# Attention scores as three products of split operands in place of one float32 product

## The reference, cut to what matters

```python
s = jnp.einsum('bqhmd,bkhmd->bhmqk', qb, kb, preferred_element_type=jnp.float32) * scale
s = jnp.where(causal, s, -jnp.inf)
prob = jax.nn.softmax(s, axis=-1)
attn = prob[:, :, 0] - lam * prob[:, :, 1]
outs.append(jnp.einsum('bhqk,bkhe->bqhe', attn.astype(v.dtype), vb))
```

## Time and profile before

| | |
|---|---|
| median of 3 runs | 3677.48 us (3675.54 to 3686.17) |
| the profiled execution | 3677.04 us, its span 3675.3 us |
| PE busy | 3268.1 us, 89% of the span |
| DVE, ACT, POOL busy | 1364.8, 978.2, 864.1 us |
| mean granted TensorE clock | 0.95 of full |
| attention stage, from the first load's issue to the last scores | about 782 to 1245 us of the span |

### The profile page before, as it was taken

The page is one execution under the profiler, slowest core; times in us unless marked ns, Lnnn a source line. Parts: engine busy times, 40 slices in busy tenths (PEclk is TensorE's granted clock), DMA queues, the critical chain, the costliest instruction groups (busy, mean ns, idle before and its releaser), DMA issues. The chain is left out here.

```text
span 3675.3 us, 70085 instructions
## 1 busy us (share of the span) xinstructions
PE 3268.1 (89%) x26336; PEld 2299.8 (63%) x26337; DVE 1364.8 (37%) x2425; ACT 978.2 (27%) x2040; POOL 864.1 (24%) x1064
## 2 busy tenths in 40 slices
PE   7999999988998578888885996799999999998799
PEld 5767878856666367777774885444444444444687
DVE  4334751036777444454443334311111111111565
ACT  3331210026777433333332111000000000000332
POOL 1001320002241467767662000000000000000343
PEclk9999999999999789999998997799999999999899
DMA  5444356360000212211112666246857665772443
GB/s 161 166 169 166 133 191 232 141 175 25 8 15 7 84 48 73 76 60 60 60 37 88 211 219 234 104 183 238 313 201 258 252 256 209 260 261 112 149 146 114
DMA packets 229220, 541.66 MB, mean 147 GB/s; under 512 B 26192, under 2 KB 62160, under 8 KB 220784
## 3 DMA queue, kind: packets, MB, share of 16 engines
q1 hardware_dynamic: 210656, 471.48, 36.5%
q0 software_dynamic: 11552, 41.95, 3.3%
q10 hardware_dynamic: 6768, 24.64, 1.6%
HBM read 408.52 MB, written 129.51 MB: 146 GB/s over the span
## 5 line engine op out<-in xcount | busy, mean ns | idle before, releaser
L559 PE MATMUL p_z<-w_in_part,hn_split 128*128 128x512 f32 x2304 | 537.5, 394 | 8.5 <-DVE w_in_part L388 4.5
L559 PEld LDWEIGHTS p_z<-w_in_part,hn_split 128*128 128x128 f32 x2304 | 434.3, 190 | 99.7 <-issue 4.8
L2311 PE MATMUL pe_gate<-w_gate_sb,e_xT 128*128 x752 | 336.4, 601 | 15.8 <-DMA w_down_sb<-in_w_down_dram 10.9
L2321 PE MATMUL pe_y<-w_down_sb,e_hT 128*128 x752 | 330.6, 592 | 1.2 <-DVE e_hT L2254 1.2
L2311 PE MATMUL pe_up<-w_up_sb,e_xT 128*128 x752 | 330.4, 592 | 0.0
L2271 DVE TENSOR_TENSOR e_h<-e_silu,pe_up 128x512 f32<-128x512 f32 x47 | 32.3, 687 | 622.9 <-issue 484.1
L2311 PEld LDWEIGHTS pe_up<-w_up_sb,e_xT 128*128 128x128 f32 x752 | 142.9, 190 | 179.9 <-issue 179.9
L2311 PEld LDWEIGHTS pe_gate<-w_gate_sb,e_xT 128*128 128x128 f32 x752 | 141.0, 193 | 178.5 <-issue 178.5
L2321 PEld LDWEIGHTS pe_y<-w_down_sb,e_hT 128*128 128x128 f32 x752 | 139.2, 190 | 158.8 <-issue 158.8
L2199 POOL COPY e_idx<-row_tokens 128x1 uint32 (+1 forms) x48 | 8.8, 183 | 973.0 <-PE pe_xT L2284 914.1
L1665 PE MATMUL pd_out<-d_w_out_part,d_mixT 128*128 128x512 f32 x768 | 187.8, 400 | 11.9 <-DVE d_w_out_part L1658 11.9
(11 more groups left out here) (412 smaller groups left out, 5544.3 us busy)
## 6 DMA issues: line engine op xcount, KB each, us to landing
w_gate_sb<-in_w_gate_dram SPq DMA_DIRECT2D x32, 2048.0 KB, 11.5
w_up_sb<-in_w_up_dram SPq DMA_DIRECT2D x32, 2048.0 KB, 16.4
w_down_sb<-in_w_down_dram SPq DMA_DIRECT2D x32, 2048.0 KB, 22.1
hn_split<-s_hT SPq DMA_DIRECT2D x48, 1024.0 KB, 5.1
s_y<-e_y ACTq DMA_DIRECT2D x47, 512.0 KB, 8.9
s_hT<-hn_split SPq DMA_DIRECT2D x16, 1024.0 KB, 6.5
s_y<-d_zeros SPq DMA_DIRECT2D x16, 1024.0 KB, 6.5
s_zr<-z_stage SPq DMA_DIRECT2D x48, 256.0 KB, 2.0
```

The costliest lines, as they stand in the source:

```text
L559: last = nc.tensor.matmul(bank, hs[m % 3][:, a, k, :].bitcast(F32R), w_part(c, b)[:, k, :].bitcast(F32R), start=(k == 0 and a == b == 0), ...
L2311: last = nc.tensor.matmul(bank[:], xT[:, k, :], w[:, bass.ds(slot, 1), k, :].rearrange("p o n -> p (o n)"), start=(k == 0), stop=(k == KD ...
L2321: last = nc.tensor.matmul(p_y[:, half, :], hT[:, k, :], wd[:, bass.ds(slot, 1), k, half * BANK:(half + 1) * BANK].rearrange("p o n -> p (o ...
```

## The change

The projection writes q and k turned and already split: ACT writes the high part of both halves (two casts of 128x512 in place of one copy), DVE subtracts it from the PSUM tile to get the low part (two subtractions in place of one copy), and SP stores four transfers of 256 KB for each tile in place of two. The low part uses the room of `attn_gain`, which is no longer read then. The attention stage loads both parts of q and k, five tensors in place of three, and each score product becomes three products of float32r parts.

```diff
-        qkT = sb("qkT_stage", [P, 8, P])
+        qkT_h = sb("qkT_stage", [P, 8, P])
+        qkT = [qkT_h[:], gain[:].rearrange("p (k n) -> p k n", k=8)]
...
-                for n, name, rdy, out in ((0, "qT", qkTa, qT_out), (4, "kT", qkTd, kT_out)):
-                    sp.wait_ge(rdy, i + 1)
-                    sp.dma_start(t[name][i * P:(i + 1) * P, :], qkT[:, n:n + 4, :].rearrange("p h n -> p (h n)")).then_inc(out, 16)
+                for n, name in enumerate(("qT", "kT")):
+                    sp.wait_ge(qkTd, 2 * i + n + 1)
+                    for k in range(2):
+                        sp.dma_start(t[name][k, i * P:(i + 1) * P, :], qkT[k][:, 4 * n:4 * n + 4, :].rearrange("p h n -> p (h n)")).then_inc(qkT_out[n], 16)
...
-            def q_turned(i):
+            def turned_high(i):
                 act.wait_ge(qkT_psum, i + 1)
-                act.wait_ge(qT_out, 16 * i)
-                nc.scalar.copy(qkT[:, 0:4, :], pT[:, 0, :].rearrange("p (k n) -> p k n", k=4)).then_inc(qkTa, 1)
+                for n in range(2):
+                    act.wait_ge(qkT_out[n], 32 * i)
+                    high_part = qkT[0][:, 4 * n:4 * n + 4, :].bitcast(F32R)
+                    nc.scalar.copy(high_part, pT[:, n, :].rearrange("p (k n) -> p k n", k=4)).then_inc(qkTa, 1)
...
-            def k_turned(i):
-                dve.wait_ge(qkT_psum, i + 1)
-                dve.wait_ge(kT_out, 16 * i)
-                nc.vector.tensor_copy(qkT[:, 4:8, :], pT[:, 1, :].rearrange("p (k n) -> p k n", k=4)).then_inc(qkTd, 1)
+            def turned_low(i):
+                for n in range(2):
+                    dve.wait_ge(qkTa, 2 * i + n + 1)
+                    part = lambda k: qkT[k][:, 4 * n:4 * n + 4, :].bitcast(F32R)
+                    nc.vector.tensor_tensor(part(1), pT[:, n, :].rearrange("p (k n) -> p k n", k=4), part(0), ALU.subtract).then_inc(qkTd, 1)
...
-        kT = sb("kT_all", [P, HEADS, TILES, P]); qT = sb("qT_all", [P, HEADS, TILES, P])
+        kT = sb("kT_all", [P, 2, HEADS, TILES, P]); qT = sb("qT_all", [P, 2, HEADS, TILES, P])
...
-                sp.dma_start(kT[:, h, a:b, :], rows_of("kT", h, a, b)).then_inc(k_in[n], 16)
-                sp.dma_start(qT[:, h, a:b, :], rows_of("qT", h, a, b)).then_inc(k_in[n], 16)
-                sp.dma_start(v[:, h, a:b, :], rows_of("v", h, a, b)).then_inc(v_in[n], 16)
+                for k in range(2):
+                    sp.dma_start(kT[:, k, h, a:b, :], rows_of(t["kT"][k], h, a, b)).then_inc(k_in[n], 16)
+                    sp.dma_start(qT[:, k, h, a:b, :], rows_of(t["qT"][k], h, a, b)).then_inc(k_in[n], 16)
+                sp.dma_start(v[:, h, a:b, :], rows_of(t["v"], h, a, b)).then_inc(v_in[n], 16)
...
-                def product(m, a, b, stop):
-                    r = slice(DH * m, DH * m + DH)
+                def product(m, a, b, n_, stop=False):
+
+                    r, (kq, kk) = slice(DH * m, DH * m + DH), PARTS[n_]
                     k0 = (EDGE[g][c] + a) // P
-                    return nc.tensor.matmul(out[:, m, a:b], qT[r, h, ROW[g], :], kT[r, h, k0:k0 + (b - a) // P, :], start=True, stop=stop)
+                    return nc.tensor.matmul(out[:, m, a:b], qT[r, kq, h, ROW[g], :].bitcast(F32R), kT[r, kk, h, k0:k0 + (b - a) // P, :].bitcast(F32R),
+                                            start=n_ == 0, stop=stop and n_ == 2)
...
                 if w <= BANK:
-                    for m in range(2):
-                        last = product(m, 0, w, not diag)
+                    for n_ in range(3):
+                        for m in range(2):
+                            last = product(m, 0, w, n_, not diag)
...
-                    tail = product(0, BANK, w, not diag)
+                    for n_ in range(3):
+                        tail = product(0, BANK, w, n_, not diag)
...
-                    product(1, mid, w, not diag)
-                    product(0, 0, BANK, True)
+                    for n_ in range(3):
+                        product(1, mid, w, n_, not diag)
+                        product(0, 0, BANK, n_, True)
                     pe.wait_ge(tail_done, sum(W[x][y] > BANK for x, y in PAIRS[:n]) + 1)
-                    last = product(1, 0, mid, True)
+                    for n_ in range(3):
+                        last = product(1, 0, mid, n_, True)
```

More of the change, by code:

```diff
@@ L120, in phase_project @@
         sq_done = sem("A_qk_sq"); qss_done = sem("A_qk_ss"); qrs_done = sem("A_qk_rstd"); rot_done = sem("A_rot")
-        qkT_psum = sem("A_qkT_psum"); qkTa = sem("A_qT"); qkTd = sem("A_kT"); qT_out = sem("A_qT_out"); kT_out = sem("A_kT_out")
+        qkT_psum = sem("A_qkT_psum"); qkTa = sem("A_qT"); qkTd = sem("A_kT"); qkT_out = [sem(f"A_qkT_out{n}") for n in range(2)]
         l1_done = sem("A_l1"); l1_act = sem("A_l1_act"); l1T_psum = sem("A_l1T_psum"); l1T_sb = sem("A_l1T")
@@ L139, in landing @@
         def landing(n):
-            room = (qsq, by_cos, by_sin, qkT) if n < 3 * W_PIECES else (x_sb[0], x_sb[1], hT[0], hT[1])
+            room = (qsq, by_cos, by_sin, qkT_h) if n < 3 * W_PIECES else (x_sb[0], x_sb[1], hT[0], hT[1])
             room = room[n % W_PIECES][:]
@@ L251, in _ @@
                 sp.wait_ge(out_dma[s], 16 * sum(n % Z_STAGES == s for n in STAGED.values()))
-            sp.wait_ge(qT_out, 16 * TILES)
-            sp.wait_ge(kT_out, 16 * TILES)
+            for n in range(2):
+                sp.wait_ge(qkT_out[n], 32 * TILES)
         @block.gpsimd
@@ L368, in _ @@
                 if i >= 1:
-                    q_turned(i - 1)
+                    turned_high(i - 1)
                 for n in pieces_after(1, i):
@@ L375, in _ @@
                 if i == 0:
-                    q_turned(TILES - 1)
+                    turned_high(TILES - 1)
                 for n in pieces_after(2, i):
@@ L511, in rotate @@
                 if i >= 1:
-                    k_turned(i - 1)
+                    turned_low(i - 1)
                 dve.drain()
@@ L526, in _ @@
                 if i == 0:
-                    k_turned(TILES - 1)
+                    turned_low(TILES - 1)
                 for n in pieces_after(2, i):
@@ L590, in turn_qk @@
                 pe.wait_ge(rot_done, i + 1)
-                pe.wait_ge(qkTa, i)
-                pe.wait_ge(qkTd, i)
+                pe.wait_ge(qkTd, 2 * i)
                 for g in range(8):
@@ L911, in scores @@
                 diag = c == CH[g] - 1
-                pe.wait_ge(k_in[part(h, ROW[g])], 32)
+                pe.wait_ge(k_in[part(h, ROW[g])], 64)
                 if n >= 2:
                     pe.wait_ge(exp_done, 2 * n - 2)
-                def product(m, a, b, stop):
-                    r = slice(DH * m, DH * m + DH)
+                def product(m, a, b, n_, stop=False):
+                    r, (kq, kk) = slice(DH * m, DH * m + DH), PARTS[n_]
                     k0 = (EDGE[g][c] + a) // P
-                    return nc.tensor.matmul(out[:, m, a:b], qT[r, h, ROW[g], :], kT[r, h, k0:k0 + (b - a) // P, :], start=True, stop=stop)
+                    return nc.tensor.matmul(out[:, m, a:b], qT[r, kq, h, ROW[g], :].bitcast(F32R), kT[r, kk, h, k0:k0 + (b - a) // P, :].bitcast(F32R),
+                                            start=n_ == 0, stop=stop and n_ == 2)
                 def add(m, what):
@@ L2594, in block_kernel @@
         t["semctx"] = ctx
-        t["v"] = dram("s_v", [SEQ, RW]); t["qT"] = dram("s_qT", [SEQ, RW]); t["kT"] = dram("s_kT", [SEQ, RW])
+        t["v"] = dram("s_v", [SEQ, RW]); t["qT"] = dram("s_qT", [2, SEQ, RW]); t["kT"] = dram("s_kT", [2, SEQ, RW])
         t["zr"] = dram("s_zr", [SEQ + 1, QKV]); t["lo"] = dram("s_lora", [3, SEQ, RW]); t["mix"] = dram("s_mix", [SEQ, D])
```

4 lines of the change are left out of this document (2 added, 2 removed).

## The result

The changed kernel takes 3690.97 us (median of 6 runs, 3688.11 to 3694.90), the kernel before 3678.44 us (6 runs on the same chip, 3674.43 to 3686.24): a ratio of 1.0032, 95% interval 1.0018 to 1.0047. It is slower by 12.5 us. The profiled execution took 3688.11 us, its span is 3686.3 us, 11.0 more than before.

The account below looks back on a forecast made before the run. PE has the most work, but load bytes set the end of an attention-stage standstill (the hole). 3677.0 us + 28.5 for loads - 13 for score products, projection nothing, gives 3692.5 us; range 3682 to 3708.

Parts of the forecast that it names:

- What bounds the kernel: Attention stage: PE fullest but not alone on the path; its 826.4 to 834.2 us standstill (the hole) ends by load bytes.
- Term 1, the loads: Attention stage loads grow from 12 to 20 MB, stores queue behind them, the hole ends later: 28.5 us cost.
- Term 2, PE's part: Attention scores: three split products cost PE less than one plain; 27.8 us less 8.8 for short ones leaves 19.0 us.
- Term 2, what of it counts: Of PE's gain, 17.5 us falls behind the hole; less 4.4 in groups of three chunks, 13 us shortens the kernel.
- Term 3, the projection: Projection: DVE's two subtractions add 0.66 us, covered by its 2.20 us wait for POOL: no time added.
- the likeliest case: Whole kernel: 3692.5 us, own range 3686 to 3697 with savings of 8 to 19 us; chance 0.52.
- The short split products: Rival, attention scores: short split products take as long as plain ones, PE gains nothing, kernel 3705 us; chance 0.2.
- The full gain: Rival, attention stage: loads hide and the chain at group ends shrinks with PE; 28.5 - 25.5, 3680 us; chance 0.15.
- The maps still run side by side: Rival, attention scores: both maps' split products no longer overlap, 60 us more after the hole, 3766 us; chance 0.05.
- The hole didn't stay: Rival, attention stage: loads don't end the hole, it stays as it is, 13 us gain remains, 3664 us; chance 0.04.

Follow-up runs that it names:

- the pair without a hole: Changed kernel and kernel before, each with the loads of heads 1 to 3 issued between output stores (groups 9, 20, 41): 3658.19 and 3671.57 us.
- products alone: Changed kernel loading only the high parts of q and k, with all three score products made from them: 3703.17 us, ratio 1.0063.
- The kernel with one product: Changed kernel with loads issued between the output stores and only the high x high product of each score: 3648.09 us, one run.
- loads alone, by more bytes: Kernel before, loading k and q of every head a second time into a buffer that nothing reads: 3708.09 us, ratio 1.0076.

## Why the prediction was right, and where it wasn't

The forecast was 3692.5 us, the result is 3691.0. That the number came out so close is partly luck: of the gain of 13 us only 8 to 9 came, and the expert stage, which had no term, gave some 7 back. The mechanism of the loads was right.

- **What bounds the kernel: right.** The end of the hole goes by the bytes of the loads. The kernels with more bytes and plain products show it twice, and the kernels with the loads between the stores have no hole.
- **Term 1, the loads, +28.5 us: right.** The hole ended 27.9 us later, the first store was issued at 853.58 (forecast about 854) and the hole ended at 862.05 (863). In totals it costs 26 to 28 us. By the 358 GB/s of the Trainium skill, page "DMA: Bandwidth & Descriptors", section "Specifications", it would be an estimated 23.4 us, which is too few.
- **Term 2, PE's part, 19.0 us: right.** Before, PE was busy 177.5 us with scores, after 158.8, 18.7 less. Behind the hole PE's busy time fell from 363.0 to 347.0 us, where 17.5 were counted.

```profile
L919 PE MATMUL p_scores<-kT_all,qT_all 64*128 64x512 f32 (+3 forms) x768 | 177.5, 517 | 14.3 <-DVE ident_half L827 13.9
```

```profile
L925 PE MATMUL p_scores<-kT_all,qT_all 64*128 64x512 f32 (+3 forms) x1152 | 158.8, 365 | 14.9 <-DVE ident_half L832 14.5
```

- **Term 2, what of it counts, -13 us: too much.** The step that failed is "In groups of one and two chunks I count PE's gain in full, since DVE's waits of 63 us for scores leave it room." The stage gave back 8.6 us, and 8.1 in the pair without a hole, about half of the 16 us that PE saved in either. How much of the shortfall is the clock? Behind the hole it fell in both profiles. Before, it was 0.86 in group 14 and 0.76 in group 46 (groups counted from 0), which took 12.58 and 14.51 us from one reciprocal to the next; in the five profiles of plain products whose clock stayed full there, both take 11.4. After, it was 0.86 to 0.88 in groups 14, 15 and 16: 12.39, 13.47 and 13.66 us, where groups of the same rows at full clock in this profile or in "products alone" take 11.19, 11.93 and 11.85. So an estimated 4.4 us before and 4.5 after are the clock's, and it leaves the 8.6 us as they are.

  Head 3 ran at the full clock in both profiles and shows where the rest went. Its six groups of two chunks, before and after (columns as in the earlier trace rows):

```profile
1175.31:1222.08 46.77, 42.60 (x277) 30.23 (x275) 35.49 (x81) 36.27 (x93) 11.66 (x24) 1.00 0.03 9
```

```profile
1196.05:1241.66 45.61, 40.55 (x313) 33.15 (x312) 35.49 (x81) 36.52 (x93) 11.67 (x24) 1.00 0.03 9
```

  PE saved 2.05 us and the groups 1.16; the forecast counted 2.3 (7,296 columns x 0.40 ns, less 4 short tails of 0.158 us). The six groups of one chunk gave 0.28 us where 0.76 were counted, and the four of three chunks 0.98 where 0.60 were. So it is the groups of one and two chunks, counted in full, that fell short, and in none of the three kinds did all of PE's saving come through. The waits behind the hole after the change (for the earlier trace rows):

```profile
PE p_attnT L960 <- DVE prob L883: 37.0, 44, 1.8
DVE neg_max L851 <- PE p_scores L929: 36.2, 20, 3.5
DVE neg_max L849 <- PE p_scores L925: 20.0, 23, 2.2
```

PE waits for `combine` 44 times where it waited 32 times, 37.0 us where it was 30.3, while DVE's two largest waits for scores fell by only 6.6 us, from 62.8 to 56.2. In head 2, whose rows rise, its six groups of two chunks went from 42.57 to 41.92 us: 0.65 us of the 1.98 that PE saved there, while PE's waits for `combine` in them rose from 1.4 to 3.0 us. So DVE's waits for scores were no room in which all of PE's gain could come through; part of it came out as PE's wait for DVE in the same groups. The kernel with one product goes further the same way: 42 us less PE work, 12 us less time, and a lower clock as well.
- **Term 3, the projection, nothing: right.** A tile takes 11.79 us as before (PE's transposes start at 484.75 and 496.54), and DVE's wait for POOL shrank from 2.20 us to 1.61, the cover that was named:

```profile
486.69 1.06 ACT L361 CAST qkT_stage<-p_hT 128x512 fp32r<-128x512 f32 x2
491.86 1.28 DVE L495 TENSOR_TENSOR attn_gain<-p_hT,qkT_stage 128x512 fp32r<-128x512 f32 x2
494.74 1.23 DVE L520 TENSOR_TENSOR lora_in<-lora_in,qk_rstd 128x1024 f32<-128x1024 f32 x1 [1.61 <-POOL qk_rstd L273]
```

- **What had no term: -7 us in the expert stage**, from the length of the program. Without it the total would have been near 3698, just above the likeliest case's own range of 3686 to 3697.
- **The rivals.** The short split products are not at the plain price: the 640 pair fell from 1.35 to 1.29 us. The full gain didn't come. The maps still run side by side. The hole didn't stay.

## What to carry to other kernels

Ask of each transfer what is queued behind it, and put the price of added bytes where that queue is waited for. Here 8 MB cost 28 us because the output stores stood behind them; issued between the stores, some 50 us ahead of their use, the same loads left one wait of about 1 us, while the one issued as the last short groups of a head ran left one of 9 us. Where two engines wait for each other in turn, a gain in one counts in part: here about half of the first 16 us and a quarter of the next 42. So find out for every kind of group which wait ends last rather than set one sum of waits against another. When two profiles are compared, look at the clock of each stretch first: one fall in one group was worth 1 to 3 us here, up to about a third of the gain that was looked for. A stage that no edit touches can still move by 0.2% with the length of a program: before a small difference is put down to an edit, read the stages that it doesn't touch.

## What was not expected of the hardware

- **Program length and weight loads.** 384 more PE records, wherever they stand, and 2 MB loads 1,000 us away land after 21.1 us and not 22.1; the expert stage of 47 blocks takes about 1021 and not about 1030 us.
- **The clock falls in places where PE stands more.** Before, it fell twice behind the hole, between 885 and 891 us (0.72), where PE had been busy 1.65 of 3 us as it fell, and right after 6 us in which PE was busy 4.08 us:

```profile
1099.00:1105.00 6.00, 4.08 (x30) 3.34 (x30) 5.47 (x12) 5.33 (x14) 0.00 (x0) 0.97 0.00 0
1105.00:1111.00 6.00, 6.00 (x23) 4.17 (x22) 1.93 (x5) 2.07 (x6) 1.94 (x4) 0.50 0.04 11
```

  PE's longest wait around either fall was 1.7 us, for DVE. PE's busy time alone doesn't decide it. At the same place of "loads alone, by more bytes" PE was busy the same 4.08 us, and the clock stayed full:

```profile
1123.62:1129.62 6.00, 4.08 (x31) 3.34 (x31) 5.48 (x12) 5.33 (x14) 0.00 (x0) 1.00 0.00 0
1129.62:1135.62 6.00, 6.00 (x43) 4.58 (x42) 3.68 (x8) 4.06 (x11) 1.94 (x4) 1.00 0.05 14
```

  After the change it fell in three places, between 912 and 948 us (0.72, 0.72 and 0.85 in 6 us each), with one product in some twenty. The eight profiles of kernels with plain products show it in none to two groups behind the hole (none in five of them), the five with three products in two or three. That PE's savings make falls more frequent fits, but no run held PE busy to test it, and there is one profile of each kernel. The time of the whole kernel goes with it: of the kernel before's runs, the five with a mean clock of 0.953 took 3673.3 us in the mean, the seven with 0.948 took 3684.9.
- **Short split products.** Three of 128 columns take 0.55 us, where the two records of a plain product took 0.49. A record of 128 columns takes 0.296 us in the mean, so that they follow each other at about (0.55 - 0.296)/2 = 0.13 us, slower than the 0.11 that I took. The Trainium skill, page "TensorE: Matmul & The Clock Gate", section "Back-to-back issue gap", gives about 81 ns for a load and product pair at 128 columns. This trace is slower than that.
